# A decoder trunk on one Trainium2 core: lending the weights' buffers at finer points, and loading one expert group by halves of its contraction

## What is computed

```
for layer in range(2):
    hn = rms_norm(h, norm_mix[layer])
    mix = nsa_stickbreak_mixer(hn, ...) if layer == 0 else hgrn2_mixer(hn, ...)
    h = h + mix
    h = h + hier_moe(rms_norm(h, norm_ffn[layer]), ...)
return rms_norm(h, final_norm)

# hier_moe, for the experts e with combine weights cs (two of the 32 are not zero for a token)
hid = silu(einsum('sd,edf->sef', xs, w_gate)) * einsum('sd,edf->sef', xs, w_up)     # d 1024, f 256
out = einsum('sef,efd->sd', hid * cs[..., None], w_down)
```

## Time and profile before

| what | value |
|---|---|
| median of three runs | 725.71 us (723.98 to 726.44) |
| the profiled execution | 726.28 us, of it 724.5 us span |
| TensorE matmul busy | 622.4 us (86% of the span) |
| VectorE, ScalarE, GpSimd busy | 260.7, 242.9, 35.3 us |
| mean granted TensorE clock | 0.943 |
| DMA | 244.50 MB, mean 337 GB/s over the span |

### The profile page before, as it was taken

The page is one execution under the profiler, slowest core; times in us unless marked ns, Lnnn a source line. Parts: engine busy times, 40 slices in busy tenths (PEclk is TensorE's granted clock), DMA queues, the critical chain, the costliest instruction groups (busy, mean ns, idle before and its releaser), DMA issues.

```text
span 724.5 us, 10731 instructions
## 1 busy us (share of the span) xinstructions
PE 622.4 (86%) x4450; PEld 407.9 (56%) x4450; DVE 260.7 (36%) x457; ACT 242.9 (34%) x540; POOL 35.3 (5%) x64
## 2 busy tenths in 40 slices
PE   9998899999997695675999999999999976595766
PEld 7997787775552341322279987887655531341312
DVE  4556787534210010110176698652521110010102
ACT  5526555451211110110166575662411110110113
POOL 3030000000000100000000001060000000000000
PEclk9999999999998897987999999999999997887989
DMA  8969137799999999999996645579999999999993
GB/s 325 262 218 313 69 117 270 282 405 389 382 416 404 409 419 422 420 421 422 405 386 228 224 141 208 191 264 399 408 349 411 417 423 421 420 422 422 421 417 154
DMA packets 59855, 244.50 MB, mean 337 GB/s; under 512 B 4562, under 2 KB 8930, under 8 KB 39075
## 3 DMA queue, kind: packets, MB, share of 16 engines
q1 hardware_dynamic: 58544, 242.33, 85.4%
q0 software_dynamic: 768, 1.40, 0.8%
q10 hardware_dynamic: 498, 0.15, 0.1%
HBM read 242.82 MB, written 1.05 MB: 337 GB/s over the span
## 4 chain that ended last, share of the span: by engine, by line
PE 56%; DMA 28%; SPq 7%; DVE 5%; ACT 2%; issue 1%; DVEq 0%; POOL 0%; POOLq 0%; ACTq 0%
DMA ring<-in_moe_w_down 24%; PE psum L1865 6%; PE psum L2262 6%; PE psum L2329 6%; DMA ring<-in_moe_w_up 4%; PE psum L1876 3%; PE psum L1869 3%; SPq L545 3%; PE psum L1874 3%; PE psum L1867 3%; PE psum L2255 3%; SPq L504 2%; PE psum L2410 2%; PE psum L2412 2%; PE psum L2411 2%; SPq L512 2%
## 5 line engine op out<-in xcount | busy, mean ns | idle before, releaser
L2262 PE MATMUL psum<-arena,xT 128*32 128x512 f32 x512 | 65.3, 668 | 34.6 <-DMA arena<-in_moe_w_up 34.6
L2262 PE MATMUL psum<-ring,xT 128*32 128x512 f32 x480 | 66.6, 682 | 32.9 <-DMA ring<-in_moe_w_up 32.9
L1593 DVE TENSOR_TENSOR arena<-psum,arena 128x256 f32<-128x256 f32 x16 | 6.8, 425 | 241.1 <-ACT arena L1072 241.1
L2329 PE MATMUL psum<-ring,arena 128*32 128x512 f32 x456 | 61.0, 619 | 12.9 <-DMA ring<-in_moe_w_down 12.8
L1068 ACT ACTIVATE arena<-psum 128x256 f32<-128x256 f32 x16 | 6.1, 384 | 195.6 <-PE psum L2262 195.6
L2255 PE MATMUL psum<-arena,xg 128*128 128x128 f32 x512 | 61.5, 278 | 0.8 <-DVE arena L1579 0.8
L2255 PEld LDWEIGHTS psum<-arena,xg 128*128 128x128 f32 x512 | 59.4, 194 | 2.7 <-issue 2.7
L2262 PEld LDWEIGHTS psum<-arena,xT 128*32 128x32 f32 x512 | 16.8, 121 | 77.1 <-issue 41.2
L2242 PE MATMUL psum<-xT,arena 128*128 128x512 f32 x128 | 57.9, 595 | 0.0
L1865 PE MATMUL psum<-x_hi,w_hi 128*128 128x256 f32 x216 | 53.9, 288 | 0.7 <-issue 0.3
L2262 PEld LDWEIGHTS psum<-ring,xT 128*32 128x32 f32 x480 | 15.2, 123 | 66.5 <-DMA ring<-in_moe_w_up 33.6
(11 more groups left out here) (353 smaller groups left out, 1049.4 us busy)
## 6 DMA issues: line engine op xcount, KB each, us to landing
ring<-in_moe_w_down SPq DMA_DIRECT2D x54, 1024.0 KB, 20.0
ring<-in_moe_w_up SPq DMA_DIRECT2D x32, 1024.0 KB, 17.2
arena<-in_moe_w_gate SPq DMA_DIRECT2D x32, 1024.0 KB, 20.4
arena<-in_moe_w_up SPq DMA_DIRECT2D x32, 1024.0 KB, 23.2
ring<-in_moe_w_gate SPq DMA_DIRECT2D x30, 1024.0 KB, 17.4
ring<-in_rec_w_in SPq DMA_DIRECT2D x16, 1024.0 KB, 13.6
ring<-in_att_w_in SPq DMA_DIRECT2D x8, 1024.0 KB, 10.8
ring<-in_att_w_out SPq DMA_DIRECT2D x4, 1024.0 KB, 16.3
```

What stands on the lines that cost most here:

```text
L2262: return pe.matmul(bank(GATE_UP)[e * CAP:(e + 1) * CAP, :].rearrange("p (w f) -> p w f", w=2), gatheredT[:, k, e * CAP:(e + 1) * CAP], w, ...
L2329: last = pe.matmul(down_bank(c)[e * CAP:(e + 1) * CAP, :], hidT[:, j, e * CAP:(e + 1) * CAP], down_part(l, kind, e, j)[:, c * 512:(c + 1) ...
```

## The change

1. Layer 0: `before_query` moves into slot 2 and `later_own` out of it, so slots 2 and 3 come free separately. SP loads slot 2 after `sb_z_raw` (all scores are computed) and slot 3 after `sb_pv`.
2. Layer 1: `square_rec` moves from `r2` to `xg`, so `r2` (slot 3, second half) is loaded after `a_psum`; `a_used` is now raised by the last matmul of `inside(1)` and frees `rA` and `rv`; `r3` waits for `o_psum`; `rC` and `r1` for `recT_psum` as before.
3. Quad 0: `first_gate_up(l, 0)` and `(l, 1)` both stand between the halves of `gather`; VectorE's copy of blocks 4 to 7 is split in two, each with its own wait, and the second half of the gather writes two banks in place of one.
4. Quad 3 is loaded by halves of the contraction: eight loads of 512 KiB once quad 1's matmuls have passed the middle (`first_used`), eight more once they are done (`gate_up >= 2`). A row of such a load is 4 KiB in a partition, and was 8 KiB.
5. The down half `last_half(l, 0)` of quad 1 now stands behind all of quad 3; down of quad 2 follows at once for three experts, and for the fourth after `down >= 2`.

```
@@ layer 0 loads
                     load_lent(sp, 0, 0, s["xg_done"], TT)
+                    sp.wait_ge(s["sb_z_raw"], SB_H)
+                    load_gate_up(sp, 0, 1, 1, 2)
                     sp.wait_ge(s["sb_pv"], SB_H)
-                    for e in (2, 3):
-                        load_gate_up(sp, 0, 1, 1, e)
+                    load_gate_up(sp, 0, 1, 1, 3)
@@ layer 1 loads
                     load_gate_up(sp, 1, 1, 1, 0, (1,))
+                    sp.wait_ge(s["a_psum"], 4)
+                    load_gate_up(sp, 1, 1, 1, 3, (1,))
                     sp.wait_ge(s["a_used"], 1)
                     load_gate_up(sp, 1, 1, 1, 0, (0,))
+                    load_gate_up(sp, 1, 1, 1, 2, (0,))
+                    sp.wait_ge(s["o_psum"], TT)
                     load_gate_up(sp, 1, 1, 1, 1, (1,))
-                    load_gate_up(sp, 1, 1, 1, 2, (0,))
                     sp.wait_ge(s["recT_psum"], 4)
                     load_gate_up(sp, 1, 1, 1, 2, (1,))
-                    load_gate_up(sp, 1, 1, 1, 3)
+                    load_gate_up(sp, 1, 1, 1, 3, (0,))
@@ quad 3 and the down weights behind it
-                later_quad(3, 3, 1, 2, third=True)
+                def quad_by_halves(half, e):
+
+                    for i, w in enumerate((moe_w_gate, moe_w_up)):
+                        c = slice(half * KD // 2 * FF, (half + 1) * KD // 2 * FF)
+                        sp.dma_start(gate_up_slots(l, 1)[e][:, i * KD * FF:(i + 1) * KD * FF][:, c],
+                                     w[l].rearrange("(q e) (p r) f -> q e p (r f)", e=QE, p=P)[3][e][:, c])\
+                            .then_inc(s[f"gate_up_loaded{l}_1" if half else "cmp_w1_rest"], 16)
+
+                sp.wait_ge(s["first_used"], 4 * (l + 1))
+                for e in range(QE):
+                    quad_by_halves(0, e)
+                sp.wait_ge(s[f"gate_up{l}"], 2)
+                for e in range(QE):
+                    quad_by_halves(1, e)
+                sp.wait_ge(s[f"down{l}"], 1)
+                load_down_half(sp, last_half(l, 0), l, 1, 0, s["ahead_loaded"])
+                load_down(sp, l, 2, range(QE - 1))
+                sp.wait_ge(s[f"down{l}"], 2)
+                load_down(sp, l, 2, range(QE - 1, QE))
                 later_quad(4, 4, 0, 3)
@@ TensorE: quad 0, and the signal from the middle of quad 1
-                gather(l, 0, between=lambda: first_gate_up(l, 0), first=True)
-                for c in range(1, KD // 2):
+                gather(l, 0, between=lambda: [first_gate_up(l, c) for c in range(KD // 4)], first=True)
+                for c in range(KD // 4, KD // 2):
                     first_gate_up(l, c)
...
+                    if front and k == KD // 2 - 1:
+                        last.then_inc(s["first_used"], 1)
@@ TensorE: down
                 elif early:
-                    pe.wait_ge(s[f"down_loaded{l}"], 80 + 16 * n)
+                    pe.wait_ge(s[f"down_loaded{l}"], 80)
                     if n:
-                        pe.wait_ge(s["ahead_loaded"], 80 * (l + 1))
+                        pe.wait_ge(s["ahead_loaded"], 96 * (l + 1))
```

More of the change, by code:

```diff
@@ L254, in hybrid_trunk @@
         kbT = a(4, T)
+        before_query = a(P)
+        assert a.at <= 3 * UW, a.at
+        a.at = 3 * UW
         vb = a(TT, SB_H * DH)
@@ L265, in hybrid_trunk @@
         later_all = a(P)
+        later_own = a(P)
         ident_r_at = a.at
@@ L301, in hybrid_trunk @@
         e_gate = rC.rearrange("p h t -> p (h t)").rearrange("p (t d) -> p t d", t=TT)
-        square_rec = r2.rearrange("p h t -> p (h t)")[:, 0:D]
+        square_rec = xg[:, 0, :]
         def rounded(name, shape, place, at=0):
@@ L379, in gather_bank @@
         def gather_bank(k, first):
-            return bank(GATHER + (k in (2, 3) if first else k // 4))
+            return bank(GATHER + (k // 2 % 2 if first else k // 4))
         def rows_hi(p):
@@ L637, in _ @@
                     if e < QE - 1:
-                        sp.wait_ge(s["first_used"], 3 * l + e + 1)
+                        sp.wait_ge(s["first_used"], 4 * l + e + 1)
                     else:
@@ L641, in _, with later_quad @@
                     load_gate_up(sp, l, 2, 0, e, (0, 1) if e else (1,))
-                def later_quad(n, q, parity, ended, third=False):
+                def later_quad(n, q, parity, ended):
                     sp.wait_ge(s[f"gate_up{l}"], n - 1)
@@ L1056, in gathered @@
                 if not first:
-                    act.wait_ge(s[f"gathered{l}"], 2 * n + 2)
+                    act.wait_ge(s[f"gathered{l}"], 2 * n + 3)
                 for k in range(KD // 2):
@@ L1582, in gathered @@
             def gathered(l, n, q, first=False, front=False):
[L1583 to L1586, removed]
+                if first:
+                    for i in range(2):
+                        dve.wait_ge(s[f"gathered{l}"], 3 + i)
+                        ks = slice(4 + 2 * i, 6 + 2 * i)
+                        dve.tensor_tensor(gatheredT[:, ks, :], gather_bank(4 + 2 * i, True)[:, 2 * i * P:2 * (i + 1) * P]
+                                          .rearrange("p (k c) -> p k c", k=2), spread(gain_ffn[:, l, ks], 2, P), ALU.mult)\
+                            .then_inc(s[f"gatheredT{l}"], 1 if i else GATHERED_PARTS - 1)
+                else:
+                    dve.wait_ge(s[f"gathered{l}"], 2 * n + 4)
+                    dve.tensor_tensor(gatheredT[:, 4:8, :], gather_bank(4, False).rearrange("p (k c) -> p k c", k=4),
+                                      spread(gain_ffn[:, l, 4:8], 2, P), ALU.mult)\
+                        .then_inc(s[f"gatheredT{l}"], GATHERED_PARTS if front else 1)
                 dve.wait_ge(s[f"slots{l}"], n + 1)
@@ L2256, in gather @@
                                          slots[:, t].rearrange("p e c -> p (e c)"), start=(t == 0), stop=(t == TT - 1))
-                    if k % 4 == 3 or first and k == 1:
+                    if k % 4 == 3 or first and k % 2:
                         last.then_inc(s[f"gathered{l}"], 1)
@@ L2276, in first_gate_up, with later_gate_up @@
                 last.then_inc(s["first_used" if c < KD // 2 - 1 else f"gate_up{l}"], 1)
-            def later_gate_up(l, n, parity, in_h=False, front=False):
+            def later_gate_up(l, n, parity, in_h=False, front=False, halves=False):
                 if front:
@@ L2283, in later_gate_up @@
                     pe.wait_ge(s[f"gatheredT{l}"], GATHERED_PARTS * (n + 1))
+                if halves:
+                    pe.wait_ge(s["cmp_w1_rest"], 32 + 128 * (l + 1))
                 pe.wait_ge(s[f"gate_up_loaded{l}_{parity}"], 64 * (n + parity))
@@ L2334, in down, with body @@
                             last.then_inc(s[f"down{l}" if c else f"down_front{l}"], 1)
-            def body(l, n, parity, early=False):
+            def body(l, n, parity, early=False, halves=False):
                 gather(l, n, busy=True)
@@ L2340, in body @@
                 turn_hidden(l, n - 1)
-                later_gate_up(l, n, parity, in_h=early)
+                later_gate_up(l, n, parity, in_h=early, halves=halves)
                 down(l, n - 1, early=early)
@@ L2359, in experts @@
                 body(l, 2, 0, early=True)
-                body(l, 3, 1)
+                body(l, 3, 1, halves=True)
                 pe.wait_ge(s["passes_ready"], l + 1)
@@ L2479, in inside @@
                     d = slice(hd * P, (hd + 1) * P)
-                    pe.matmul(acc[:, d], aMv[:, t * RH + hd, :], rv[:, t, d], start=(hd % 4 == 0), stop=True,
-                              skip_group_check=True)
+                    last = pe.matmul(acc[:, d], aMv[:, t * RH + hd, :], rv[:, t, d], start=(hd % 4 == 0), stop=True,
+                                     skip_group_check=True)
+                if t:
+                    last.then_inc(s["a_used"], 1)
             def carried(t, *chunks):
```

11 lines of the change are left out of this document (2 added, 9 removed).

## The result

| kernel | median us (lowest to highest) | ratio to before |
|---|---|---|
| before, 8 runs beside the change | 724.80 (723.36 to 726.44) | |
| the change, 8 runs | 728.14 (727.14 to 730.13) | 1.0052 [1.0039, 1.0065] |

Forecast were 722.7 us and faster. The change is slower by 3.3 us, more than the 0.3% that can be told, and inside the range; the time is close to that of the rival "slower, by the new wait" (728.9). The profiled execution took 728.42 us (span 726.7), 2.1 us more than the profiled one before (726.28); the rest of the 3.3 us is spread between executions.

What follows compares the result with a forecast made beforehand. Expert weight loads were taken to bound the kernel, with room where a plateau begins. Net gains of 1.8 us (layer 0) and 1.2 us (layer 1) sum to 3.0 us: 722.7 us against the median 725.71; range 719 to 728.5.

Steps and rivals of the forecast that it cites:

- slower, by the new wait: Rival: quad 1's down half lands late, delaying quad 2's fourth down load and all behind it; 728.9 us, chance 0.17.
- What bounds the kernel: On the experts' plateaus the weight stream (405 to 423 GB/s) bounds; seven low slices ahead of each plateau leave room.
- The gains ahead of the experts: Layer 0 before the experts: slot 2 loaded earlier, most swallowed by `load_first(3)` at 144.44; gain 1.5 us, worst case 0.
- 1.5 + 0.6 us in layer 0: Layer 0: 1.5 us from lending slot 2 earlier, 0.6 us from reordered quad 0 freeing its second piece earlier.
- 0.7 + 1.9 us in layer 1: Layer 1: 0.7 us left of earlier slot loads at quad 2's first piece, 1.9 us from its piece issued at 530.41.
- What the halves cost: Quad 3's 8 MiB in 4 KiB rows move at 394 GB/s against 424; 1.5 us lost in each layer.
- The wait: TensorE waits 8 us in layer 0, 7 in layer 1, at quad 1's `down` for its last half load.
- The hole is 0.6 us: Layer 0: queue empty from 224.0, when quad 2's three down loads end, until its fourth gets going at 224.6.
- Layer 0 is ahead by 1.8 us: Layer 0's net gain: the last 3.75 us of quad 2's down bytes begin at 224.6, before the change at 226.4.
- Ahead by 1.3 us: Layer 1's net gain: fourth down load goes at 578.4, before at 579.7; rounded down to 1.2 for a small hole.
- Fixed costs for each load: Rival: 16 more loads, eight in each layer, each pay an empty queue's 2.3 us; 37 us, 762 us, chance 0.01.
- The clock: After TensorE's idle wait, quad 1's 32 `down` matmuls run at a lowered clock, 6.2 us where they took 3.51.

Runs made afterwards that it cites:

- e11_change_again: The change itself, unchanged, run again for a second profile; 728.53 us, ratio 1.0047.
- e9_wait_without_hole: The change, with experts 0 and 1 of quad 4 (4 MiB) issued before SP waits for the fourth down load of quad 2; 722.94 us, ratio 0.9975.
- e1_lend_only: Parts 1 to 3 of the change alone, quad 3 and the down weights as in the kernel before; 722.85 us, ratio 0.9968.
- lending nor order alone: The kernel before with only parts 1 and 2 (lending): 724.68 us; with only part 3 and the old lending waits (order): 724.20 us.
- e2_half_early: The change, with quad 1's down half moved to right after the first expert's second halves of quad 3; 722.66 us, ratio 0.9968.
- e7_two_by_halves: The change, with only experts 0 and 1 of quad 3 by halves, then the down half, then experts 2 and 3 whole; 721.48 us, ratio 0.9945.
- e5_all_4k_rows: The kernel before, with every gate and up load outside quad 0 as two 512 KiB loads with 4 KiB rows; 730.59 us, ratio 1.0071.
- e3_halves_only: Parts 4 and 5 of the change alone on the kernel before; 730.36 us, ratio 1.0065.
- e6_all_two_dmas_8k: The kernel before, with gate and up loads outside quad 0 cut by partitions (64 and 64), rows still 8 KiB; 950.75 us, ratio 1.2961.

## Why the prediction was wrong

**What bounds the kernel** was right, though the reading of the earlier trace rows was loose: eight slices, not seven, are low in layer 0 and six in layer 1, and single slices of the plateaus lie at 349 to 399. All that follows is in bytes of the plateau.

**The gains ahead of the experts** came, but at about half of their size. Slot 2's loads went at 123.37 and landed at 138.3 (138.5 had been said), the queue ran empty from 143 (48 GB/s in 143 to 146), as said, so most of the lent 2 MiB was swallowed by the fixed issue of `load_first(3)`. The low rate at 190 to 194 went from 309 to 408 GB/s. By 197 the bytes were ahead by 2.2 us; 3.6 us less what the halves had cost by then had been forecast. But two more traces with the same code up to there are ahead by 1.1 us (`e11_change_again`, 374 GB/s) and 0.4 us (`e9_wait_without_hole`, 370). Layer 1 was ahead by 0.8 us at 552. The prediction gave parts 1 to 3 1.5 + 0.6 us in layer 0 and 0.7 + 1.9 us in layer 1, 4.7 us; `e1_lend_only`, which has just these, kept 2.4 us to the end, and its interval (1.3 to 3.3 us) leaves 4.7 out. Which of the four terms was too large no run tells; that neither lending nor order alone gave a clear gain fits with smaller ones throughout.

**What the halves cost** had been put at 1.5 us in each layer, from 394 GB/s. The rate over 198 to 212 was 390, where "near 400" had been said, but the kernel before moves only 409 there, so this is 0.6 us; the 371 GB/s of 198 to 206 did not come again (392 in the second trace of the change; 395 in the kernel before). In layer 1 the low rate is plain: 368 GB/s in 555 to 563 (375 in the second trace) against 425 before, 1.1 us. Its reason held only in part. Rows of 4 KiB alone give 413 GB/s, 0.37 us for 8 MiB. In the 8 us after 555 the change and `e2_half_early` moved 368 where `e7_two_by_halves` moved 422, which is 1.0 us. Why eight second halves in a row are slower than the same rows with both halves side by side, as in `e5_all_4k_rows`, no run tells.

**The wait** came as forecast, and `down` ended earlier than said: the half landed at 215.1 and 571.4 (216.5 and 570.2), TensorE waited 7.5 and 7.9 us (8 and 7), `down` ended at 220.2 and 577.5 (222.7 and 576.4). With these times my own rule would leave the queue full: in layer 0 the fourth load gets going at 222.2, and the three before it would end at 215.1 + 7.5 = 222.6.

**The step that failed is "The hole is 0.6 us", and with it "Layer 0 is ahead by 1.8 us" and "Ahead by 1.3 us".** I let the three down loads start when the half before them had landed. But much of them had been moved by then. From the half's landing to the fourth issue the queue moved 405 x 5.1 = 2.07 MB in layer 0 and 351 x 6.1 = 2.14 MB in layer 1, of the 3.15 MB that I put there, and in layer 1 it was almost empty at the end. So about 1 MiB, 2.5 us, was already through. (I had said myself that a landing is that of the last engine; that the other engines had gone on to the down loads would explain this, but no row here shows single engines.) The same slip made the landings of before into starts ("so they began at 226.4"). The fourth load now lands at 220.2 + 7.0 = 227.2, 3 us before the last down load of the kernel before, and by landings the change looks ahead; by bytes it is behind. The true holes cost 1.6 and 2.7 us, the second of them beyond the 2 us that I had named as proof against me. About 0.8 us more was lost behind it in layer 0 (226 to 260: 398 against 408 GB/s). It lies in 248 to 254; the window and the line of GpSimd's small loads there, in the kernel after:

```profile
248.00:254.00 6.00, 5.07 (x36) 1.29 (x40) 0.00 (x0) 0.00 (x0) 0.03 (x1) 0.72 1.01 347
...
q0 software_dynamic: 127, 0.09, 16.7%
```

Before, this stretch moves 418 GB/s and has none of these loads. Their 0.09 MB took 16.7% of the engines' time (5.3% in the second trace of the change, with 392 GB/s), and (418 - 347) x 6 / 421 = 1.0 us. Why they took so much there no run tells.

Set against the forecast of 3.0 us ahead, the 3.3 us behind are a miss of 6.3 us. The late parts cost 5.1 us (`e3_halves_only`) where 4.7 - 3.0 = 1.7 us follow from the forecast, 3.4 us more; the holes, 4.3 us in the traces of the change for 0.7 us forecast, are enough for that. The early parts gave 2.3 us less than said. The remaining 0.6 us is within the spread.

**The rivals.** The slower one named the place, the mechanism and nearly the time (728.9), with a chance of 0.17. That its number came so near is luck in part: it supposed that the early gains do not reach quad 3 and that the halves land at 220.1 and 572.8. Its condition was off by the same slip: it asked for a landing after 218.2 and 571.5, and the loss came with 215.1 and 571.4. What spoke against it, "4 us of slack come from the three down loads that are released early", was worth 2.5 us less. Fixed costs for each load (762 us) are refuted by `e5_all_4k_rows`. The Trainium skill ("DMA: Bandwidth & Descriptors", section "Bandwidth") asks for loads of at least 1 MiB; here 512 KiB loads in a full queue cost 2% of the rate (413 against 421 GB/s).

**The clock.** I gave much care to the lowered clock behind TensorE's idle time. It came: 32 matmuls took 5.02 and 6.08 us instead of 3.51. `e9_wait_without_hole` shows that this mattered only through the moment at which SP was released, and not at all once SP had other loads to issue.

## What to carry to other kernels

Where transfers bound a stretch, ask at each wait of the issuing queue how many bytes are still queued when it is reached and how many are left when it ends. Count bytes and not landings: when a load landed here, about 1 MiB of what stood behind it had already been moved. A load whose consumer releases further loads goes early in the order, or gets loads behind it that need no release. Here an idle TensorE in such a stretch (7.3 us) cost nothing that could be seen as long as the queue stayed fed.

## What was unexpected of the hardware

Loads over 64 partitions moved little more than half the rate with all engines reported busy. Windows of `e6_all_two_dmas_8k` (its profiled execution took 957.93 us):

```profile
200.00:212.00 12.00, 0.63 (x3) 0.20 (x2) 0.00 (x0) 0.66 (x2) 0.00 (x0) 0.68 1.02 243
137.00:148.00 11.00, 10.89 (x47) 8.53 (x46) 5.63 (x6) 2.65 (x6) 0.00 (x0) 1.00 1.02 232
```

The share is 1.02, as at 421 GB/s, and 243 and 232 GB/s are moved. The same bytes as halves of columns over all 128 partitions ran at 413. A full share of the DMA engines therefore does not say that they move what they can.

SP's issues get longer in a run of many loads. SP's timeline of the kernel after:

```profile
189.96 0.45 SPq L661 DMA_DIRECT2D arena<-in_moe_w_gate  x1
190.45 1.18 SPq L661 DMA_DIRECT2D arena<-in_moe_w_up  x1
191.68 1.06 SPq L661 DMA_DIRECT2D arena<-in_moe_w_gate  x1
```

The first nine half loads took 0.33 to 0.46 us each to issue, the seven behind them 1.05 to 1.18 us. It would be handy to read this as the sign of a full queue, but the rows don't bear it out: the kernel before issued its last loads of quad 3 in 0.45 to 0.55 us each, and the last of them landed 21.5 us later. What sets the length no run tells.
